# Projecting the neighbourhood's values with tokens stationary, and loading them by strips from device memory

## The reference

```
proj = rmsnorm(x) @ w_in                    # 1024 -> 2304 columns
qa, ka, va, qb, kb, vb = split(proj)        # 512, 128, 128, 512, 512, 512
oa = window_attention(rotary(qa), rotary(ka), va)    # 8 query heads, 2 key heads, blocks of 128
ob = neighbourhood_attention(qb, kb, vb)    # 8 heads, grid 64 columns wide
x  = x + concat(norm(oa), norm(ob)) @ w_out
x  = x + expert_choice_swiglu(rmsnorm(x))   # 16 experts
y  = rmsnorm(x)
```

## Time and profile before

| | |
|---|---|
| median of 3 runs | 2661.93 us (2661.03 to 2663.06) |
| the profiled execution | 2664.18 us |
| its span, first to last instruction | 2662.4 us |
| busy: TensorE, VectorE, ScalarE, GpSimd | 94%, 65%, 56%, 7% |
| projection | to about 333 us |
| attention | about 334 to 588 us |

### The profile page before, as it was taken

How to read it: one execution, slowest core, us unless ns; L and a number is a source line. 1 busy time by engine, 2 the same in 40 slices (tenths; PEclk the granted TensorE clock), 3 DMA queues, 4 the chain that set the end, 5 groups by cost and what they waited for, 6 DMA issues and landing times. The chain is left out here.

```text
span 2662.4 us, 42232 instructions
## 1 busy us (share of the span) xinstructions
PE 2515.5 (94%) x15538; PEld 2229.5 (84%) x15538; DVE 1731.1 (65%) x2743; ACT 1486.1 (56%) x2124; POOL 187.2 (7%) x268
## 2 busy tenths in 40 slices
PE   7999999979965999999999999999999999999992
PEld 5888866657755998999989999899998999989991
DVE  6354277765577766767667676676766767667675
ACT  4333277765543565655656556565565655656553
POOL 0000011000001010110101101011010110101100
PEclk9999999989987999999999999999999999999996
DMA  4332132235435676776767767677676776767765
GB/s 151 127 127 90 62 108 92 89 117 184 144 121 184 234 246 227 253 248 232 246 227 253 248 232 246 227 253 248 231 246 227 252 248 231 246 227 253 249 230 209
DMA packets 95484, 536.65 MB, mean 202 GB/s; under 512 B 10608, under 2 KB 15472, under 8 KB 44848
## 3 DMA queue, kind: packets, MB, share of 16 engines
q1 hardware_dynamic: 88016, 509.72, 54.2%
q0 software_dynamic: 7392, 25.96, 4.5%
HBM read 497.89 MB, written 37.75 MB: 201 GB/s over the span
## 5 line engine op out<-in xcount | busy, mean ns | idle before, releaser
L1413 DVE TENSOR_TENSOR ex_w_lo<-ex_w,ex_w_hi 128x2048 fp32r<-128x2048 f32 x387 | 887.0, 2292 | 471.1 <-ACT ex_w_hi L1366 471.1
L1366 ACT ACTIVATE ex_w_hi<-ex_w 128x2048 fp32r<-128x2048 f32 x387 | 739.2, 1910 | 232.2 <-PE ex_down_ps L1517 114.1
L1499 PE MATMUL ex_gate_ps<-ex_xt,ex_w_hi 128*128 128x384 f32 x2048 | 594.3, 360 | 1.5 <-DVE ex_xt L1419 1.5
L1499 PE MATMUL ex_up_ps<-ex_xt,ex_w_hi 128*128 128x384 f32 x2048 | 592.1, 359 | 0.0
L1501 PE MATMUL ex_gate_ps<-ex_xt,ex_w_lo 128*128 128x192 f32 x2048 | 513.8, 251 | 0.0
L1501 PE MATMUL ex_up_ps<-ex_xt,ex_w_lo 128*128 128x192 f32 x2048 | 512.7, 250 | 0.0
L1501 PEld LDWEIGHTS ex_gate_ps<-ex_xt,ex_w_lo 128*128 128x128 f32 x2048 | 392.5, 192 | 0.6
L1501 PEld LDWEIGHTS ex_up_ps<-ex_xt,ex_w_lo 128*128 128x128 f32 x2048 | 391.2, 191 | 0.0
L1499 PEld LDWEIGHTS ex_gate_ps<-ex_xt,ex_w_hi 128*128 128x128 f32 x2048 | 386.0, 188 | 2.3 <-issue 1.7
L1499 PEld LDWEIGHTS ex_up_ps<-ex_xt,ex_w_hi 128*128 128x128 f32 x2048 | 384.6, 188 | 0.0
L1386 ACT ACTIVATE ex_up_low<-ex_up_ps 128x384 f32<-128x384 f32 x128 | 63.0, 492 | 213.6 <-PE ex_up_ps L1501 213.6
(11 more groups left out here) (215 smaller groups left out, 4142.1 us busy)
## 6 DMA issues: line engine op xcount, KB each, us to landing
ex_w<-in_w_experts SPq DMA_DIRECT2D x387, 1024.0 KB, 4.8
pj_w<-in_w_in SPq DMA_DIRECT2D x54, 512.0 KB, 3.4
at_bias<-in_near_bias SPq DMA_DIRECT2D x8, 1536.0 KB, 8.1
pj_x<-in_x SPq DMA_DIRECT2D x12, 512.0 KB, 4.4
o_scratch<-at_o SPq DMA_DIRECT2D x24, 256.0 KB
mx_o<-o_scratch SPq DMA_DIRECT2D x12, 512.0 KB, 4.1
mx_x<-in_x SPq DMA_DIRECT2D x12, 512.0 KB, 4.6
acc_scratch<-mx_x SPq DMA_DIRECT2D x12, 512.0 KB, 5.4
```

What stands on the lines that cost most here:

```text
L1366: act.activation(w_hi[:, c % SLOTS, :], w[:, c % SLOTS, :], ACT.Copy).then_inc(hi_w, 1)
L1413: dve.tensor_tensor(w_lo[:, c % SLOTS, :], w[:, c % SLOTS, :], w_hi[:, c % SLOTS, :].bitcast(F32), ALU.subtract).then_inc(lo_w, 1)
L1499: nc.tensor.matmul(out[:, b, 0:2 * CAP], w_hi[:, slot, f], xt[:, k, :, :].rearrange("p h c -> p (h c)"), start=k == 0, stop=False)
```

## The change

The neighbourhood's values are no longer kept transposed. Their last four chunks of each group hold another layout of the weights: chunk m has two slices of the depth for all 512 columns. TensorE takes 128 tokens as stationary and the 512 columns as moving, three passes for each of two slices and each of four token tiles, so 24 matmuls a chunk. The four results stand in four PSUM banks, `pj_v`, a new one, and the two banks of the other chunks. They are complete after the fourth chunk, which takes the tiles in the order 2, 3, 0, 1. ScalarE copies each to `pj_near`, and SyncE stores it to `v_scratch` in device memory: four stores of 256 KB a group, at chunk 3 of the next group, and for the last group at the end of the stage. The window's values become chunk 5.

In the attention, staging, transposes and copies are gone, and the GpSimd program with them. SyncE waits until all 12 stores have landed and loads the values of strips 0 and 1 with six loads each, and after near blocks 2 and 5 those of strips 2 and 3. A load takes 4 rows by 32 columns of 512 values, 256 KB. TensorE waits for a strip's loads before the first near block of the strip. The buffer `at_flipped` is allocated earlier, under the same size.

```diff
@@ project @@
+        near = sb("pj_near", [P, G_TILES, NEAR_WIDTH])
+        near_ps = [v_ps, ps("pj_near_ps", [P, 512])] + out_ps
...
+        LAST_ORDER = [2, 3, 0, 1]
...
+            def store_near(g):
+                for k, t in enumerate(LAST_ORDER):
+                    sp.wait_ge(near_taken, g * G_TILES + k + 1)
+                    sp.dma_start(d["v"][g * G_TILES + t], near[:, t, :]).then_inc(keep.near_stored, 16)
...
+                if n == 3 and g:
+                    store_near(g - 1)
+            store_near(GROUPS - 1)
...
-                    else:
-                        act.activation(keep.vt.at(slice(0, P), q - FIRST_V - 1, t0, GROUP), src,
-                                       ACT.Copy).then_inc(taken, 1)
+                    elif q == CHUNKS - 1:
+                        if g:
+                            act.wait_ge(keep.near_stored, 16 * G_TILES * g)
+                        for k, t in enumerate(LAST_ORDER):
+                            if k < G_TILES - 1:
+                                act.wait_ge(near_done, g * (G_TILES - 1) + k + 1)
+                            else:
+                                act.wait_ge(chunk_done, i)
+                            act.activation(near[:, t, :], near_ps[t][:], ACT.Copy).then_inc(near_taken, 1)
...
+                    else:
+                        m = n - TURNED
+                        if m == 0:
+                            pe.wait_ge(v_copied, g + 1)
+                            if g:
+                                pe.wait_ge(near_taken, g * G_TILES)
+                        for t in LAST_ORDER if m == VB - 1 else range(G_TILES):
+                            if m == 0 and t >= 2:
+                                pe.wait_ge(taken, taken_with(g * CHUNKS + TURNED - 4 + t))
+                            c = slice(t * P, (t + 1) * P)
+                            for j in range(2):
+                                k = 2 * m + j
+                                hi, lo = (x[:, s, 4 * j:4 * j + 4, :].rearrange("p j c -> p (j c)") for x in (w_hi, w_lo))
+                                last = three_pass(nc, near_ps[t][:], (x_hi[g][:, k, c], x_lo[g][:, k, c]), (hi, lo),
+                                                  k == 0, k == DT - 1)
@@ attend @@
-        v_stage = sb("at_v_stage", [P, 2, PAIRS, P])
-        v_ps = ps("at_v", [P, 512])
+        v_in = [sem(f"at_v_in{i}") for i in range(2)]
...
+            def load_values(strip):
+                for i, (group, row) in enumerate(V_TILES):
+                    first = group // GRID_W + row
+                    rows = d["v_grid"][first:first + V_ROWS, KEY_COL[strip]:KEY_COL[strip] + K_COLS, :]
+                    sp.dma_start(v_near[:, (len(V_TILES) * strip + i) % V_SLOTS, :], rows).then_inc(v_in[strip % 2], 16)
...
+            sp.wait_ge(keep.near_stored, 16 * TILES)
+            load_values(0)
+            load_values(1)
             for bi, b in enumerate(blocks):
                 sp.wait_ge(scaled, PAIRS * (bi + 1))
...
+                    if b.kind == 2 and b.strip + 2 < STRIPS:
+                        load_values(b.strip + 2)
...
-                    pool.tensor_copy(v_stage[:, n % 2, c, :].rearrange("p (r c) -> p r c", c=K_COLS),
-                                     src[:, :, KEY_COL[strip]:KEY_COL[strip] + K_COLS]).then_inc(v_staged, 1)
...
-                    act.activation(v_near[:, n % V_SLOTS, :], v_ps[:], ACT.Copy).then_inc(v_copied, 1)
...
-                        pe.wait_ge(v_copied, len(V_TILES) * (b.strip + 1))
+                        pe.wait_ge(v_in[b.strip % 2], 16 * len(V_TILES) * (b.strip // 2 + 1))
...
-                    for c in range(PAIRS):
-                        last = nc.tensor.transpose(v_ps[:, c * P:(c + 1) * P], v_stage[:, n % 2, c, :],
-                                                   ident[:])
@@ program @@
+    d["v"] = nc.dram_tensor("v_scratch", [TILES, P, NEAR_WIDTH], F32, kind="Internal").ap()
+    d["v_grid"] = d["v"].rearrange("t (r c) e -> (t r) c e", c=GRID_W)
```

More of the change, by code:

```diff
@@ L42 @@
 KEY_ROWS = 8
-QA, KA, QB, KB = 4, 1, 4, 4
-V_CHUNKS = 5
+QA, KA, VA, QB, KB = 4, 1, 1, 4, 4
 ROTATED = QA + KA
-CHUNKS = QA + KA + QB + KB + V_CHUNKS
-FIRST_V = CHUNKS - V_CHUNKS
+FIRST_QB = ROTATED + VA
+FIRST_KB = FIRST_QB + QB
+TURNED = FIRST_KB + KB
+VB = 4
+CHUNKS = TURNED + VB
+NEAR_WIDTH = 512
 TURN = [p + ROT_HALF if p < ROT_HALF else p - ROT_HALF if p < 2 * ROT_HALF else p for p in range(32)]
@@ L92, with __init__ @@
 class Heads:
-    def __init__(self, q, k, v, vt, x1_hi, x1_lo):
-        self.q, self.k, self.v, self.vt = q, k, v, vt
+    def __init__(self, q, k, v, flipped, x1_hi, x1_lo, near_stored):
+        self.q, self.k, self.v, self.flipped = q, k, v, flipped
         self.x1_hi, self.x1_lo = x1_hi, x1_lo
+        self.near_stored = near_stored
 class Route:
@@ L208, in project, with taken_with @@
         v_copied = sem("pj_v_copied")
+        near_done = sem("pj_near_done")
+        near_taken = sem("pj_near_taken")
         block = ctx.enter_context(nc.Block())
         N = GROUPS * CHUNKS
+        def taken_with(i):
+            g, n = divmod(i, CHUNKS)
+            return g * TURNED + n + 1
+        LAST_ORDER = [2, 3, 0, 1]
         def next_tile(i, after):
@@ L388, in _ @@
                 g, q = divmod(i - 2, CHUNKS)
-                if q == FIRST_V and g < GROUPS:
+                if q == ROTATED and g < GROUPS:
                     dve.wait_ge(v_turned, g + 1)
@@ L422, in _ @@
                     s = i % W_SLOTS
-                    for j in range(DT):
-                        last = three_pass(nc, out_ps[i % 2][:], (w_hi[:, s, j, :], w_lo[:, s, j, :]),
-                                          (x_hi[g][:, j, :], x_lo[g][:, j, :]), j == 0, j == DT - 1)
+                    if n < TURNED:
+                        if n >= 2:
+                            pe.wait_ge(taken, taken_with(i - 2))
+                        elif g:
+                            pe.wait_ge(near_taken, (g - 1) * G_TILES + n + 1)
+                        for j in range(DT):
+                            last = three_pass(nc, out_ps[i % 2][:], (w_hi[:, s, j, :], w_lo[:, s, j, :]),
+                                              (x_hi[g][:, j, :], x_lo[g][:, j, :]), j == 0, j == DT - 1)
+                    else:
[13 more added lines that the diff above has]
+                                                  k == 0, k == DT - 1)
+                            if m == VB - 1 and t != LAST_ORDER[-1]:
+                                last.then_inc(near_done, 1)
                     last.then_inc(chunk_done, 1)
                 g, q = divmod(i - 1, CHUNKS)
-                if q == FIRST_V:
-                    pe.wait_ge(taken, i)
+                if q == ROTATED:
+                    pe.wait_ge(taken, taken_with(i - 1))
                     if g:
                         pe.wait_ge(v_copied, g)
+                        pe.wait_ge(near_taken, g * G_TILES)
                     for t in range(G_TILES):
@@ L442 @@
 WINDOW_KEYS = 3 * P
+FLIPS = 6
 PAIRS = 4
@@ L506, in attend @@
         near_start = {b.number: PAIRS * bi for bi, b in enumerate(blocks) if not b.window}
[L508 to L515, removed]
+        PROBS, STATS, BIASES, V_SLOTS, SCORES = 6, 4, 3, 2 * len(V_TILES), 3
         bias = sb("at_bias", [P, BIASES, 2 * PAIRS, NEAR_KEYS])
@@ L775, in _ @@
                     last.then_inc(weighed, 1)
[L776 to L781, removed]
-                        last = nc.tensor.transpose(v_ps[:, c * P:(c + 1) * P], v_stage[:, n % 2, c, :],
-                                                   ident[:])
-                    last.then_inc(v_turned, 1)
 S_ROUNDS, P_ROUNDS = S_CAP // 8, P_CAP // 8
@@ L1619, in program @@
         q_s, k_s = sb("q_s", [P, QA + QB, S_TOK]), sb("k_s", [P, KA + KB, S_TOK])
-        v_s, vt_s = sb("v_s", [P, S_TILES, P]), sb("vt_s", [P, V_CHUNKS - 1, S_TOK])
+        v_s = sb("v_s", [P, S_TILES, P])
+        near_stored = outer.enter_context(nc.semaphore("near_stored"))
         with ExitStack() as early:
@@ L1625, in program @@
         q_p, k_p = sb("q_p", [P, QA + QB, P_TOK]), sb("k_p", [P, KA + KB, P_TOK])
-        v_p, vt_p = sb("v_p", [P, TILES - S_TILES, P]), sb("vt_p", [P, V_CHUNKS - 1, P_TOK])
-        keep = Heads(Tokens(q_s, q_p), Tokens(k_s, k_p), Values(v_s, v_p), Tokens(vt_s, vt_p), x1_hi, x1_lo)
+        v_p = sb("v_p", [P, TILES - S_TILES, P])
+        flipped = sb("at_flipped", [P, FLIPS, NEAR_KEYS])
+        keep = Heads(Tokens(q_s, q_p), Tokens(k_s, k_p), Values(v_s, v_p), flipped, x1_hi, x1_lo, near_stored)
         project(nc, d, keep)
@@ L1652, in columns @@
     out = [span(qa0 + HD * c, HD) + span(qa0 + HD * (c + 4), HD) for c in range(QA)]
-    out += [span(ka0)]
+    out += [span(ka0), span(va0)]
     out += [span(qb0 + P * c) for c in range(QB)] + [span(kb0 + P * c) for c in range(KB)]
-    out += [span(va0)] + [span(vb0 + P * c) for c in range(V_CHUNKS - 1)]
-    return np.array(out)
+    return np.array(out), np.array(span(vb0, NEAR_WIDTH))
```

(6 more changed lines are left out.)

50 lines of the change are left out of this document (11 added, 39 removed).

## The result

The changed kernel takes 2677.35 us (median of 4 runs, 2677.26 to 2678.4); the kernel before took 2662.49 beside it (4 runs, 2661.03 to 2663.29). The ratio is 1.0055, with a 95% interval of 1.0042 to 1.0068: slower by 14.9 us, where 7.1 was forecast. The profiled execution took 2678.4 us with a span of 2676.3, which is 13.9 more than the span before.

What follows compares the result with a forecast made beforehand. TensorE, busy 94% of the span, was taken to bound the kernel. Terms: 14 - 10.1 + 2.7 + 0.5 = +7.1 us on the median 2661.93, so 2669.0 us; own range 2663.4 to 2674.9, whole range 2647 to 2677.

Steps and rivals of the forecast that it cites:

- The first wait: Attention, scaling of unit 8: VectorE waits for block 0's store until 381.7; with half clock +14 us (11.5 to 16).
- The 18 steps: Attention, near blocks 0 to 8: removing these value steps saves 10.1 us of TensorE's time (9.5 to 10.5).
- A: Attention: value loads use all sixteen engines, or the store does not queue behind them; no waits, 2650.0 us; chance 0.19.
- B: Attention: each value load also pays a slow start of 0.7 us, lengthening the waits; 2686 us; chance 0.05.
- C: Projection: bank changes every six matmuls drop the clock to 0.50; +65 us, 2734 us; chance 0.02.
- The +0.5 for the new chunks: Projection: value chunks with tokens stationary and weights moving cost 0.5 us more (0 to 2.0).
- Waits of 1.3 and 2.0 us, less VectorE's idle 0.28 in a unit: +2.7 (0.5 to 4.5): Attention, after near blocks 2 and 5: window blocks' stores land behind six loads, later than their buffer is needed; +2.7 us.
- the 24.4 of the forecast: Attention, after near blocks 2 and 5: the window block's store lands 24.4 us after the near block's store is issued.
- The mechanism behind the store's lateness: Attention: block 0's store, issued at about 354, stands behind all twelve loads on four engines and lands at 381.3.

Runs made afterwards that it cites:

- both forms of the kernel before: The kernel before the change with its two output buffers (2662.49 us beside the changed kernel), and the same with four output buffers (2663.83 us, ratio 1.0002).
- the last run: The changed kernel with four output buffers in place of two and each value load cut into one-row loads: 2653.49 us, ratio 0.9962 to the kernel before.

## Why the prediction was right in direction and too small in size

**What held.** The change is slower by 14.9 us where 7.1 was forecast, and that is above the forecast's own range of 1.5 to 13. Most of the mechanism held all the same. The loads run on four engines (0.26 to 0.28, 97 to 100 GB/s; 98 forecast). The first wait stands at the scaling of unit 8, for the store of block 0, and ends at 382.20 (381.7 forecast), in half clock. In the ticks it is +14.7 us (+14 forecast): unit 11 comes at 389.87 for 375.78, which is +14.09, and one value step of 0.58 had been saved in between. The 18 steps are worth 10.5 (10.1 forecast, bounds 9.5 and 10.5), as the run with four buffers shows cleanly: from -1.45 to -11.97. The 0.4 too little comes from the earlier trace rows, which set a tick with a step beside that of another unit without one, 2.50 - 2.04. The same unit without its step takes 1.94 (475.00 - 473.06 with four buffers), so a step costs 0.56 there too.

Rivals A, B and C all fell: A by the share, B because six and twelve loads flow at 97 to 100 GB/s without a pause, C because the projection's matmuls with moving weights have a mean of 389 to 400 ns, those with moving tokens 389 to 394. The +0.5 for the new chunks should have been 0: the projection ends at the same time (its last matmul starts at 332.21, before at 332.23) at a granted clock of 1.00. The first score comes 0.4 us later, at 337.05 for 336.62.

**The step that failed: "Waits of 1.3 and 2.0 us, less VectorE's idle 0.28 in a unit: +2.7 (0.5 to 4.5)".** The two later waits cost 7.8 us, above the upper bound. From the ticks: (4.99 - 2.57) + (2.71 - 2.57) = 2.6 after near block 2, and (6.25 - 2.57) + (3.60 - 2.57) + (3.05 - 2.57) = 5.2 after near block 5. The times of need were right: the scalings end their waits 25.8 us (466.73 - 440.96) and 26.3 us (525.66 - 499.37) after the near block's store is issued; less what the tick lost, 2.42 and 3.68, that is 23.4 and 22.6, for 23.4 and 22.7 forecast. Two things were wrong. The stores land 1.4 and 1.9 us later than the 24.4 of the forecast. And the clock: after the wait of 4.15 us it fell to half for a stretch, 1.5 us, which the forecast had only behind the long wait. So the two stops cost 6.1 where 2.7 was summed, and the ticks behind them grew by 1.7, 1.5 of it at half clock, where nothing was summed. Two windows, the 4 us up to the end of the second wait, and the stretch behind the third:

```profile
463.00:467.00 4.00, 1.99 (x18) 1.04 (x12) 1.07 (x6) 1.97 (x7) 0.00 (x0) 1.00 0.99 337
...
528.00:530.00 2.00, 2.00 (x9) 1.35 (x7) 1.32 (x7) 1.12 (x5) 0.00 (x0) 0.50 0.06 25
```

Why the stores land later was not isolated. The first of the windows shows a DMA share of 0.99, because near block 3's store and its bias table, issued at 461.49 and 462.17, then run beside the end of the window block's store. That they slow it down is an argument, not a finding. In the run with strip 1 later, the new wait was expected too small in the same way, by both parts.

**What the forecast did not have.** It took the rest of the program as unchanged. From the last tick of the attention to the first matmul of the experts the changed kernel takes 251.35 us, the kernel before 249.05: +2.3. In both TensorE stops once near the end of the output projection, for VectorE's low parts, equally long. In the changed kernel it is then at half clock:

```profile
773.20 0.80 PE L130 MATMUL mx_ps<-mx_w_hi,mx_m_hi 128*128 128x512 f32 x1 [2.58 <-DVE mx_m_lo L1044]
773.79 0.63 PE L131 MATMUL mx_ps<-mx_w_lo,mx_m_hi 128*128 128x512 f32 x1
774.22 0.63 PE L132 MATMUL mx_ps<-mx_w_hi,mx_m_lo 128*128 128x512 f32 x1
```

In the run with one-row loads and four buffers, whose code is the same from there on, it is not (0.24 us from one matmul to the next in the last two rows, for 0.43):

```profile
747.76 0.51 PE L130 MATMUL mx_ps<-mx_w_hi,mx_m_hi 128*128 128x512 f32 x1 [2.57 <-DVE mx_m_lo L1047]
748.10 0.40 PE L131 MATMUL mx_ps<-mx_w_lo,mx_m_hi 128*128 128x512 f32 x1
748.34 0.40 PE L132 MATMUL mx_ps<-mx_w_hi,mx_m_lo 128*128 128x512 f32 x1
```

Five of the ten traces have the drop (the changed kernel, four buffers, strip 1 later, GpSimd's stores, two-row loads), five do not (both forms of the kernel before, one-row loads, three buffers, the last run). Three of the eight traces with the change lack it, so the change doesn't bring it by itself; that neither of the two traces of the kernel before has it may be chance. What decides it is open, and so is how much of the 14.9 us of the medians is due to it.

**The mechanism behind the store's lateness** was right in effect and wrong in place. The prediction had the store "issued at 356.56, then at about 354" and waiting on the engines. It was ready at 355.4 and issued at 369.88, since SyncE's own issue was held back, and with the loads outstanding then it landed a further 12.3 us later. The end is the same, because either way it stands behind all twelve loads; that the landing was forecast to 0.9 us doesn't show that the way to it was right. It matters for the remedy: the run with GpSimd's stores shows that another queue is enough, although the engines are the same.

**The sum as measured**: +14.7 - 10.5 + 7.8 = +12.0, and the last tick of the attention shows +11.90; +2.3 in the next stage; -0.3 in the rest: +13.9 in the span. The two profiled executions differ by 14.2, the medians by 14.9.

## What to carry to other kernels

Before work is moved from an engine to a transfer, ask how many DMA engines the transfer's shape gets, and what stands behind it in the same queue: here work worth 12 us was removed, and three waits for stores of 256 KB behind slow loads took back twice that (25 us between the medians with two buffers and with four). A wait is the landing less the time of need, so a deeper buffer for the waiting side is the cheap cure. Splitting the loads into single rows does as well (splitting them into halves made it worse by 66 us), and another queue for the stores nearly (2655.7 us for 2652.3). A stop of TensorE can cost a stretch at half clock on top of its own length: here stops of 3.65 us (the changed kernel) and 4.82 us (three buffers) had one behind them, one of 2.38 us had none, and one of 2.57 us had it in half of the traces.

## What the runs showed of the hardware that was not expected

- SyncE's issue of a DMA blocks when slow transfers are outstanding: twelve loads on four engines took 32.85 us to issue, twenty-four on two engines 64.14 us. At 369.88, when the last had been issued, some 10 us of loads were still to run, about four of them at 2.67 us (an estimate from twelve loads since 348): the store behind them landed 12.3 us later.
- A transfer that GpSimd issues does not wait behind those that SyncE has outstanding on the same engines, but takes longer beside them: three stores landed 5.4 to 5.6 us after their issue with loads outstanding (at least 8 us of them for the first), and one at 395.29, after the loads, 2.3 us. A burst of bytes doesn't tell that a store has landed: it came within 3 us of the issue in either queue, and SyncE's store landed after 12.3 us.
- A source of one row of 32 columns runs on all engines (share 1.06), one of two rows on two (0.13), one of four on four (0.26).
- The same stop of 2.57 us brought a stretch at a granted clock of 0.50 in five traces and none in five others.
